# Weighted sums with high and low values in one stationary operand, in five forgetting steps and two memory steps

## The reference

```
def fox_attention(q, k, v, logcum):            # layer 1, 12 heads, blocks of 128 queries
    sc = einsum('bqhd,bkhd->bhqk', qi, k) * scale + ci[..., None] - logcum[:, :, None, :]
    p = softmax(where(kpos <= qpos, sc, -inf))
    return einsum('bhqk,bkhd->bqhd', p, v)     # the weighted sum
def memory_attention(qm, mk, mv):              # both layers, 4 heads, 256 memory tokens
    p = softmax(einsum('bshd,bmhd->bhsm', qm, mk) * scale)
    return einsum('bhsm,bmhd->bshd', p, mv)    # the weighted sum
y = concatenate([mix, mo], axis=-1) @ w_o[layer]
```

## Time and profile before

| what | value |
|---|---|
| median of 3 runs | 1149.09 us (1149.09 to 1149.47) |
| profiled execution, its own time | 1149.07 us |
| its span in the trace | 1147.3 us |
| busy: PE, weight loads, DVE, ACT, POOL | 1133.8, 958.4, 627.6, 481.7, 123.1 us |
| granted TensorE clock, mean | 0.998 |
| memory steps 0 and 1 | about 33 to 80 us |
| forgetting steps 3 to 8 | about 600 to 746 us |

### The profile page before, as it was taken

How to read it: one execution, slowest core, us unless ns; L and a number is a source line. 1 busy time by engine, 2 the same in 40 slices (tenths; PEclk the granted TensorE clock), 3 DMA queues, 4 the chain that set the end, 5 groups by cost and what they waited for, 6 DMA issues and landing times.

```text
span 1147.3 us, 16304 instructions
## 1 busy us (share of the span) xinstructions
PE 1133.8 (99%) x5768; PEld 958.4 (84%) x5768; DVE 627.6 (55%) x1085; ACT 481.7 (42%) x832; POOL 123.1 (11%) x146
## 2 busy tenths in 40 slices
PE   9999999999999999999999999999999999999997
PEld 8888899888888888889778888799888888888886
DVE  6668667543323453456687787758444223444226
ACT  6556357333112433225755555637333112343120
POOL 1200073000000000233301101055000000000000
PEclk9999999999999999999999999999999999999999
DMA  9322323333333333333212212133333333233232
GB/s 365 97 74 91 129 74 111 92 95 107 92 94 94 105 92 100 102 95 90 56 44 68 55 55 74 38 110 97 88 99 103 92 104 92 81 105 94 92 114 88
DMA packets 164231, 110.37 MB, mean 96 GB/s; under 512 B 4690, under 2 KB 156242, under 8 KB 163668
## 3 DMA queue, kind: packets, MB, share of 16 engines
q1 hardware_dynamic: 163460, 106.28, 30.7%
q10 hardware_dynamic: 720, 3.41, 0.8%
HBM read 105.48 MB, written 4.19 MB: 96 GB/s over the span
## 4 chain that ended last, share of the span: by engine, by line
PE 91%; DVE 4%; ACT 2%; issue 1%; DMA 1%; SPq 0%; DVEq 0%; ACTq 0%
PE proj L615 72%; PE pv L615 3%; PE tr L615 3%; PE sc L615 2%; PE proj L1024 2%; PE sc L1024 2%; PE pv L1024 2%; PE tr L1024 2%; PE tr L666 1%; PE proj L710 1%; DVE w_lo L1652 1%; DVE sc L1721 1%; DMA w_raw<-in_mem_w_kv 1%; ACT w_hi L1242 1%; DVE probs L1740 1%
## 5 line engine op out<-in xcount | busy, mean ns | idle before, releaser
L1652 DVE TENSOR_TENSOR w_lo<-w_raw,w_hi 128x1024 fp32r<-128x1024 f32 (+1 forms) x165 | 206.0, 1249 | 148.6 <-ACT w_hi L1242 100.5
L615 PE MATMUL proj<-x_hi,w_hi 128*128 128x512 f32 (+1 forms) x728 | 284.1, 391 | 1.0 <-DVE w_lo L1652 0.5
L615 PE MATMUL proj<-x_hi,w_lo 128*128 128x512 f32 (+1 forms) x728 | 280.0, 385 | 0.0
L615 PE MATMUL proj<-x_lo,w_hi 128*128 128x512 f32 (+1 forms) x728 | 277.8, 385 | 0.0
L1242 ACT CAST w_hi<-w_raw 128x1024 fp32r<-128x1024 f32 x150 | 156.7, 1045 | 199.8 <-PE proj L615 194.3
L615 PEld LDWEIGHTS proj<-x_hi,w_lo 128*128 128x128 f32 x728 | 136.8, 188 | 27.7
L615 PEld LDWEIGHTS proj<-x_hi,w_hi 128*128 128x128 f32 x728 | 136.9, 188 | 27.3 <-DVE w_lo L1652 1.0
L615 PEld LDWEIGHTS proj<-x_lo,w_hi 128*128 128x128 f32 x728 | 135.9, 188 | 24.7
L615 PE MATMUL proj<-h_hi,w_hi 128*128 128x512 f32 (+1 forms) x384 | 146.3, 381 | 0.4 <-DVE w_lo L1652 0.4
L615 PE MATMUL proj<-h_hi,w_lo 128*128 128x512 f32 (+1 forms) x384 | 146.0, 380 | 0.0
L615 PE MATMUL proj<-h_lo,w_hi 128*128 128x512 f32 (+1 forms) x384 | 146.0, 380 | 0.0
(11 more groups left out here) (411 smaller groups left out, 1829.1 us busy)
## 6 DMA issues: line engine op xcount, KB each, us to landing
w_raw<-in_w_up SPq DMA_DIRECT2D x64, 512.0 KB, 4.0
w_raw<-in_w_down SPq DMA_DIRECT2D x64, 512.0 KB, 3.6
w_raw<-in_w_o SPq DMA_DIRECT2D x16, 512.0 KB, 3.7
w_raw<-in_a_w_in SPq DMA_DIRECT2D x12, 512.0 KB, 3.3
w_raw<-in_kv_w SPq DMA_DIRECT2D x12, 512.0 KB, 3.9
w_raw<-in_b_w_q SPq DMA_DIRECT2D x8, 512.0 KB, 3.7
w_raw<-in_mem_w_kv SPq DMA_DIRECT2D x5, 512.0 KB, 3.7
x<-in_x SPq DMA_DIRECT2D x4, 512.0 KB, 10.3
```

What stands on the lines that cost most here:

```text
L615: last = pe.matmul(target, lhs, rhs, start=start and n == 0, stop=stop and n == len(terms) - 1)
L1652: return dve.tensor_tensor(target, whole, hi.bitcast(F32), ALU.subtract)
```

## The change

The values of a pair now lie in four quarters of 64 columns (`mv_cat`, `v_cat`): hi of head 0, lo of head 0, lo of head 1, hi of head 1, so that each head's 128 stationary columns are its own hi and lo (`both`). In memory steps 0 and 1 and in forgetting steps 3 to 7 (`stacked`) a weighted sum is two matmuls instead of three for each tile of keys: `both` by the probabilities' hi, `both` by their lo. Own rows then hold hi's share and the other 64 rows lo's share, which must be added: ACT copies the other rows to a new tile `small` (64x512), DVE makes `mix_lo` as before, and then `small` is added to `mix_lo`, by DVE itself in the memory steps, by POOL in the forgetting steps (`add_small`). `mix_ready` is raised after that addition. Step 2 and step 8 keep three matmuls; in step 8 a one-element memset of POOL raises `mix_ready`.

```diff
+        v_cat = put("v_cat", [P, 2, TT, 4 * HALF], F32R, A0 + 32 * K1)
+        small = put("small", [P, T], F32, A0 + 66 * K1)
...
+        def stacked(s):
+            return not double(s) and s.base != STEP_LAST
...
+            def value_terms(cat, head, ph, pl, two):
+                both, low = cat[:, head * P:(head + 1) * P], cat[:, HALF:3 * HALF]
+                return [(both, ph), (both, pl)] + ([] if two else [(low, ph)])
...
-                    last = products(pv[head][:, seen], [(vh, ph), (vh, pl), (vl, ph)], j == 0, j == tiles - 1)
+                    last = products(pv[head][:, seen], value_terms(v_cat[:, c, j] if fox(s) else mv_cat[:, j, c], head, ph, pl, stacked(s)),
+                                    j == 0, j == tiles - 1)
...
                 act.copy(mix_hi[rows, bass.ds(step_tile(s), 1), :], pv[head][rows, :].rearrange("p (a t) -> p a t", a=1))\
                     .then_inc(mix_hi_ready, 1)
+                if stacked(s):
+                    act.copy(small[rows, :], pv[head][other_rows(head), :]).then_inc(small_ready, 1)
...
+                last = rest(mix_lo[rows, tile, :], pv[head][rows, :].rearrange("p (a t) -> p a t", a=1), mix_hi[rows, tile, :])
+                n = stacked_at(s, head)
+                if fox(s):
+                    last.then_inc(lo_made, 1)
+                    return
+                if stacked(s):
+                    last.then_inc(lo_made, 1)
+                    dve.wait_ge(lo_made, n)
+                    dve.wait_ge(small_ready, n)
+                    last = dve.tensor_tensor(mix_lo[rows, tile, :], mix_lo[rows, tile, :].bitcast(F32),
+                                             small[rows, :].rearrange("p (a t) -> p a t", a=1), ALU.add)
+                last.then_inc(mix_ready, 1)
...
+            def add_small(s, head):
+                rows, n = slice(head * HALF, (head + 1) * HALF), stacked_at(s, head)
+                own = mix_lo[rows, step_tile(s), :]
+                pool.wait_ge(small_ready, n)
+                pool.wait_ge(lo_made, n)
+                pool.tensor_tensor(own, own.bitcast(F32), small[rows, :], ALU.add).then_inc(mix_ready, 1)
+            copy_heads(0)
+            for pair in range(1, PAIRS):
                 copy_heads(pair)
+                for head in range(2):
+                    add_small(Pos(STEP_FOX + pair - 1), head)
+            for head in range(2):
+                pool.wait_ge(lo_made, stacked_at(Pos(STEP_LAST), head))
+                pool.memset(small[0:1, head:head + 1], 0.0).then_inc(mix_ready, 1)
```

More of the change, by code:

```diff
@@ L156, in trunk_kernel @@
         mk_rest = put("mk_rest", [P, 2 * MEMPAIRS, M], F32R)
-        mv_hi = put("mv_hi", [P, MT, MEMPAIRS * P], F32R)
-        mv_lo = put("mv_lo", [P, MT, MEMPAIRS * P], F32R)
+        mv_cat = put("mv_cat", [P, MT, MEMPAIRS, 4 * HALF], F32R)
         ident = put("ident", [P, P], F32)
@@ L433, in up_bank, with quarters, value_hi, value_lo @@
             return tr[g.slot] if g.trip is None and g.base in spare else proj[g.slot]
+        def quarters(cat):
+            return cat.rearrange("p n (q d) -> p n q d", q=4)
+        def value_hi(cat):
+            return quarters(cat)[:, :, 0:4:3, :]
+        def value_lo(cat):
+            return quarters(cat)[:, :, 1:3, :]
+        def by_heads(bank):
+            return bank.rearrange("p (n h d) -> p n h d", h=2, d=HALF)
+        def mem_cat():
+            return mv_cat[:, :, :, :].rearrange("p m c x -> p (m c) x")
+        def stacked(s):
+            return not double(s) and s.base != STEP_LAST
+        def stacked_at(s, head, off=0):
+            return (s if s.base < STEP_B else s.plus(-1)).at(head + 1 + off, 2)
         def gated(j, c):
@@ L786, in attend_pair @@
                 ph, pl = double_places(pair)
-                own = slice(pair * P, (pair + 1) * P)
                 for head in range(2):
@@ L791, in attend_pair @@
                     for j in range(MT):
-                        vh, vl = mv_hi[:, j, own], mv_lo[:, j, own]
-                        last = products(pv[head][:, :], [(vh, ph[:, head, j, :]), (vh, pl[:, head, j, :]), (vl, ph[:, head, j, :])],
+                        last = products(pv[head][:, :], value_terms(mv_cat[:, j, pair], head, ph[:, head, j, :], pl[:, head, j, :], False),
                                         j == 0, j == MT - 1)
@@ L1291, in natural_values @@
                 act.wait_ge(w_used, B_MEM[0][2 + m] + 1)
-                act.copy(mv_hi[:, m], proj[G_MEM[0][2 + m] % 2][:, 0:M]).then_inc(mv_hi_ready, 1)
+                act.copy(value_hi(mv_cat[:, m]), by_heads(proj[G_MEM[0][2 + m] % 2][:, 0:M])).then_inc(mv_hi_ready, 1)
             def memory_values():
-                turned_hi(Pos(T_MV), mv_hi[:, :, :], tr[T_MV % 2][:, :].rearrange("p (m c) -> p m c", m=MT))
+                turned_hi(Pos(T_MV), value_hi(mem_cat()), by_heads(tr[T_MV % 2][:, :]))
             def memory_queries(b, g, c):
@@ L1401, in pair_step @@
                     act.wait_ge(vt_done, values.at(1))
-                    act.copy(v_hi[:, values.slot], values_bank(s)[:, :].rearrange("p (t c) -> p t c", t=TT)).then_inc(vt_hi, 1)
+                    act.copy(value_hi(v_cat[:, values.slot]), by_heads(values_bank(s)[:, :])).then_inc(vt_hi, 1)
             def squares(n, j, g):
@@ L1705, in natural_values @@
                 dve.wait_ge(mv_hi_ready, m + 1)
-                rest(mv_lo[:, m], proj[g % 2][:, 0:M], mv_hi[:, m]).then_inc(proj_free[g % 2], 1)
+                rest(value_lo(mv_cat[:, m]), by_heads(proj[g % 2][:, 0:M]), value_hi(mv_cat[:, m])).then_inc(proj_free[g % 2], 1)
             def memory_values():
-                turned_lo(Pos(T_MV), Pos(H_MV), mv_lo[:, :, :], mv_hi[:, :, :],
-                          tr[T_MV % 2][:, :].rearrange("p (m c) -> p m c", m=MT))
+                turned_lo(Pos(T_MV), Pos(H_MV), value_lo(mem_cat()), value_hi(mem_cat()), by_heads(tr[T_MV % 2][:, :]))
             def row_max(s, u):
@@ L1756, in attended @@
                 tile = bass.ds(step_tile(s), 1)
-                rest(mix_lo[rows, tile, :], pv[head][rows, :].rearrange("p (a t) -> p a t", a=1),
-                     mix_hi[rows, tile, :]).then_inc(mix_ready, 1)
+                last = rest(mix_lo[rows, tile, :], pv[head][rows, :].rearrange("p (a t) -> p a t", a=1), mix_hi[rows, tile, :])
[10 more added lines that the diff above has]
+                last.then_inc(mix_ready, 1)
             def natural_z(n):
@@ L1879, in pair_step @@
                     dve.wait_ge(vt_hi, values.at(1))
-                    rest(v_lo[:, values.slot], values_bank(s)[:, :].rearrange("p (t c) -> p t c", t=TT),
-                         v_hi[:, values.slot]).then_inc(vt_ready, 1)
+                    rest(value_lo(v_cat[:, values.slot]), by_heads(values_bank(s)[:, :]),
+                         value_hi(v_cat[:, values.slot])).then_inc(vt_ready, 1)
             def residual(n, b, g, j, first=True, target=None):
@@ L2367, in _ @@
                 layer_norm(n)
-            for pair in range(PAIRS):
-                copy_heads(pair)
+            def add_small(s, head):
[6 more added lines that the diff above has]
+            for pair in range(1, PAIRS):
+                copy_heads(pair)
+                for head in range(2):
[3 more added lines that the diff above has]
+                pool.memset(small[0:1, head:head + 1], 0.0).then_inc(mix_ready, 1)
             layer_norm(2)
```

7 lines of the change are left out of this document (1 added, 6 removed).

## The result

The changed kernel takes 1153.04 us (median of 7 runs, 1152.77 to 1153.51), the kernel before 1149.21 us beside it (7 runs, 1149.01 to 1149.71): a ratio of 1.0032, 95% interval 1.0023 to 1.0041. The change costs 3.8 us. The forecast was 1149.7, with 1152.2 as the upper end of its range: a loss of 0.6 us was forecast and 3.8 came. The profiled execution took 1152.8 us, 3.7 more than that of before; by it the forecast is 3.1 us short.

The account below looks back on a forecast made before the run. PE is 99% busy, but DVE's and ACT's chain was taken to hide part of the saving. Memory steps -0.46, steps 3 to 6 +0.4, step 7 +0.5, step 8 +0.2: +0.6 on 1149.07, forecast 1149.7 us, range 1146.0 to 1152.2.

Parts of the forecast that it names:

- Head 0's half: Forgetting steps: the 0.63 us saved in head 0's sum is worth 0, as PE waits for unit 7's `probs`.
- ACT's copy, charged 0.46 us: Forgetting steps: the copy to `small` ahead of unit 6's `pb_hi` makes that end 0.46 us later.
- The addition was sized well: Memory steps: DVE's addition to `mix_lo` taken as 0.69 us, 0.72 with its wait for itself.
- -0.23: Memory steps 0 and 1: net gain of 0.23 us per step, -0.46 for two.
- POOL's addition holds w_lo: Forgetting steps: POOL's 1.29 us addition to head 0 runs first; `w_lo` ends at 699.08 instead of 698.09.
- the forecast's signs of being wrong: `w_lo` keeps 1.22 us, POOL's addition is near 0.6, or PE reaches the next projection 0.5 us or more earlier.
- +0.09: Forgetting steps: PE's next projection starts 0.09 us later than before, at 699.85; +0.4 us over steps 3 to 6.
- The smaller form of the slower rival: Forgetting steps: first addition follows `w_lo`'s start, ends 699.6; `turn_values` waits 0.2 to 0.3 us longer; 1150.7, within chance 0.15.
- Second additions: Head 1's addition, about 701.4 to 702.7, meets the next `w_lo`; 0.1 to 0.2 us delay, covered by DVE's idle time.
- steps 7 and 8: Step 7: later `w_lo` delays step 8's first row maximum to about 728.3, +0.5 us; step 8's memset and handover, +0.2 us.
- the rival in which it lengthens the chain: Forgetting steps: head 1's addition lies across the next `w_lo`; +4 us on top, 1153.7; chance 0.15 including its smaller form.
- The second rival: Forgetting steps: POOL's addition is short or the standstill doesn't come; -0.59 us per step, -2.4 us total, 1146.7; chance 0.17.

Follow-up runs that it names:

- late_copy: bank_free with ACT's copy moved behind unit 7's `pb_hi` or behind `v_hi`, and DVE's memory-step addition behind `pa_lo`: 1146.54 us, ratio 0.9975.
- matmuls_only: Against the kernel before: two matmuls for three, without copy, addition or memsets, so the sums lack a share: 1145.78 us, ratio 0.9972.
- gap_64: Changed kernel with the first 64 of 512 columns of `kc` made before `w_lo` on DVE: 1153.06 us, ratio 1.0035.
- bank_free: Changed kernel, but DVE's subtraction raises `mix_ready`; only the output projection and ACT's next copy wait for the addition; no memsets: 1150.01 us, ratio 1.0006.
- fox_only: The change only in forgetting steps 3 to 7, memory steps as in the kernel before: 1152.06 us, ratio 1.0025.
- all_matmuls: Changed kernel with the third matmul put back everywhere, copy and additions kept: 1153.89 us, ratio 1.0040.
- gap runs: Changed kernel with the first 64 (gap_64) or 256 (gap_256) of `kc`'s 512 columns made before `w_lo`: 1153.06 and 1151.98 us.

## Why the prediction was wrong

**Head 0's half is worth 0: right.** 0.62 us per step is won by the matmuls alone, not 1.25.

**The step that failed is ACT's copy, charged 0.46 us.** "ACT's start to start for such a copy is 694.52 - 694.06 = 0.46 us": the row was that of `mix_hi`, followed by `pb_hi`. The copy to `small` takes part in two distances, 0.59 from `mix_hi` and 0.61 to `pb_hi`, so it adds 0.74. The trace of the kernel before had a warning: head 1's `mix_hi`, 699.67, is followed by `v_hi` only at 700.28, 0.61 us later with 0.58 recorded. The missing 0.28 us goes straight down the line: ACT's `pb_hi`, DVE's `pb_lo` and `mix_lo`, then `w_lo` with POOL's addition follow each other without a gap that could take it up. In the memory steps it is the same number. ACT and DVE in memory step 0, after the change:

```profile
50.71 0.57 ACT L1356 CAST mix_hi<-pv 64x512 fp32r<-64x512 f32 x1
51.31 0.58 ACT L1359 COPY small<-pv 64x512 f32<-64x512 f32 x1
51.91 0.65 ACT L1285 CAST pa_hi<-tr 128x256 fp32r<-128x256 f32 x2
```

```profile
52.66 0.67 DVE L1682 TENSOR_TENSOR mix_lo<-pv,mix_hi 64x512 fp32r<-64x512 f32 x1
53.37 0.68 DVE L1795 TENSOR_TENSOR mix_lo<-mix_lo,small 64x512 fp32r<-64x512 f32 x1
53.98 0.41 DVE L1682 TENSOR_TENSOR pa_lo<-tr,pa_hi 128x256 fp32r<-128x256 f32 x1
```

PE at the same place, after the change and, last, before it:

```profile
54.53 0.47 PE L643 MATMUL pv<-pa_hi,mv_cat 128*128 128x512 f32 x1 [0.48 <-DVE pa_lo L1682]
...
55.53 0.39 PE L643 MATMUL proj<-x_hi,w_hi 128*128 128x512 f32 x1
```

```profile
55.13 0.39 PE L615 MATMUL proj<-x_hi,w_hi 128*128 128x512 f32 x1
```

The addition was sized well (0.71 before it, 0.61 behind, where `mix_lo` alone has 0.60: it adds 0.72). `pa_lo` of unit 7 is done at 54.39, less the opening's 0.15 us 54.24; the forecast had 53.94. PE's sum starts at 54.53, less 0.15 54.38, instead of 54.0, and the projection behind it at 55.38 instead of 55.13: +0.25 us a step where -0.23 was forecast. Of these 0.48 us 0.30 is there at the end of `pa_lo`, the copy's; 0.08 is the handover to PE (0.14 instead of 0.06), and 0.08 the sum itself, 1.00 us instead of four times 0.23, its first matmul being followed after more than 0.23. In step 1 it is +0.22. So the two steps make 0.9 us of the 3.1 missed, by step 0's rows nearly two thirds of it the copy's. late_copy, where copy and addition stand behind unit 7's `pa_hi` and `pa_lo`, gets 54.65, a gain of 0.48, and matmuls_only by the same count 54.63: the copy's and the addition's place was the whole of it.

**"POOL's addition holds w_lo": wrong for the changed kernel, and of little weight for its time.** The forecast took the row in which POOL is recorded 0.21 us ahead and wins. Here POOL is recorded 0.34 or 0.35 us ahead in each of the five steps and loses, so of the forecast's signs of being wrong the first came: `w_lo` keeps its 1.2 us, and PE waits for the addition, not for `kc`. gap_64 is the mechanism as forecast, and takes the same time. So the forecast's "+0.09" must be compared with gap_64, row for row, shifted so that unit 7's transposes fall on 694.95 (77.31 us):

| event | forecast | gap_64, shifted |
|---|---|---|
| `mix_lo` ends | 696.64 | 696.92 |
| addition starts | 696.70 | 697.10 |
| addition ends | 697.99 | 698.39 |
| `w_lo` ends | 699.08 | 699.47 |
| `kc` ends | 699.79 | 700.14 |
| next projection | 699.85 | 700.28 |

0.28 us is there when `mix_lo` ends: the copy. Another 0.12 comes between `mix_lo` and the addition: the handover from DVE to POOL takes 0.18 us, and the forecast had used the 0.06 of DVE to PE. From there the chain was right to 0.05 us (`kc`'s rest is a little shorter than `kc`, its handover to PE 0.08 longer than forecast). 0.09 + 0.43 = 0.52 is the 0.5 that a step lost; over four steps 2.2 us came for 0.4. With the memory steps' 0.9 and the opening's 0.15 that is 2.9 of the 3.1.

**The smaller form of the slower rival** (the addition behind `w_lo`, `turn_values` waits) is what came. It had the addition end at 699.6 and `turn_values` 0.2 to 0.3 us later than before. Measured from unit 7's transposes, the addition ended after 702.30 - 697.46 = 4.84 us instead of 4.65, and `turn_values` started after 4.89, where it was 699.38 - 694.95 = 4.43 before: 0.46 us later. The rival was right in kind, that `turn_values` waits for an addition that stands behind `w_lo`, and short by the same copy. Its condition is not what the rows show, though: it asked for an addition that comes after `w_lo` has begun, and this one is recorded 0.35 us before it.

**Second additions: right; steps 7 and 8: right in number, in part by luck.** Head 1's addition runs from 703.95 for 1.29 us, 6.49 us after unit 7's transposes where the forecast had 6.45, and is over before the next `w_lo` starts (705.51); the rival in which it lengthens the chain falls, though its 1153.7 is the forecast nearest to 1153.04. The rest behind step 7 came to 0.72 us where 0.5 and 0.2 were forecast. Step 8's first row maximum starts at 731.32, less the 2.96 us lost before it 728.36, where about 728.3 was forecast from 727.79. But it was to come from a `w_lo` that ends 1.0 us later; `w_lo` ends 0.64 later, and it is `second_lo` behind it that stands still:

```profile
728.47 1.46 DVE L1682 TENSOR_TENSOR second_lo<-w_raw,second_hi 128x1024 fp32r<-128x1024 f32 x1
```

It is recorded at 1.46 us instead of 1.23 and ends 1.09 us after POOL's long addition (726.15 to 728.84). In gap_64, where the addition holds `w_lo` up as forecast, the same stretch is 757.92 - 711.18 = 46.74 us, 1.13 more than before (cutting `kc` in two is some of it). No experiment took the memset by itself; the 0.72 less the 0.57 of the row maximum leave 0.15 us for it.

**The second rival** (POOL holds DVE up less because 64 partitions are short work) fell: the addition of 64x512 takes 1.29 us undisturbed, as the earlier trace rows has it for 128x512.

## What to carry to other kernels

When work is taken from the engine that is busy 99% and given to idle ones, ask in which queue and in front of what it is put, and who waits for it. Above what the matmuls alone take (matmuls_only, 1145.78 us), the same copy and the same addition cost 7.3 us in the changed kernel, 4.2 when nobody waits for the addition (bank_free), and 0.8 when the copy also stands behind the probabilities (late_copy). Let each wait ask for what it needs (the bank is free) and not for what happens to be signalled last (the sum is ready). When two engines shut each other out, price both orders: the end of the pair, and what stands behind it for each. And a start-to-start distance holds for the pair of instructions that it was read from, not for one of them.

## What the runs showed of the hardware

**ACT instructions overlap or not by their neighbour.** `mix_hi` to `pb_hi` is 0.46 us from start to start with 0.57 recorded, in the earlier trace rows and in matmuls_only (615.44, 615.90); the Trainium skill (ScalarE: Activation LUTs, What ACT_TABLE_LOAD costs) states an overlap of some 93 ns for back-to-back activations, and these rows agree with 0.11. Around the copy to `small`, which reads 64 partitions and writes the other 64, there is none: 0.59 and 0.61. Nor is there any, in the kernel before, between head 1's `mix_hi` and `v_hi` (699.67 and 700.28), so the copy's change of partitions can't be the only cause. What takes it away no run tells.

**Who gets the shared port is not to be read from the recorded starts alone.** With the addition recorded 0.34 to 0.36 us ahead of a `w_lo` that follows directly on another DVE instruction, `w_lo` won, in all five steps of the changed kernel and likewise of fox_only, all_matmuls and bank_free; recorded 0.21 us ahead of one that had waited for ACT, as in the earlier trace rows, POOL won; and recorded 0.40 us ahead of one that follows directly (532.27 and 532.67 in the trace of the changed kernel), or 0.69 and more as in the gap runs, POOL won too. The Trainium skill (SBUF — State Buffer, Who interferes with whom) gives the pair to whichever instruction issues first; the traces agree if a queued DVE instruction issues some tenths before it is recorded, which is a reading and not shown. What was the same in all runs: the loser ends 1.07 to 1.15 us after the winner, and `pb_lo`, with one input in PSUM, held POOL up nowhere (619.79 to 621.08 in gap_64, beside `pb_lo` to 620.21).
